# Choosing a core's program: the role read once and first, the two long programs swapped in place

## The reference

```python
def hybrid_layer(x, mem, g_in, w_in, g_q, g_kv, w_uq, w_ukv, sinks, rel_table,
                 g_mem, w_mem_kv, w_out, cos, sin):
    h = rms_norm(x, g_in)
    (c_q, c_kv, k_pe, z_mla, q_swa, k_swa, v_swa, z_swa, q_mem, z_mem) = split_cols(h @ w_in, IN_SIZES)
    y_mla = mla_attention(c_q, c_kv, k_pe, g_q, g_kv, w_uq, w_ukv, cos, sin) * jax.nn.silu(z_mla)
    y_swa = swa_attention(q_swa, k_swa, v_swa, sinks, rel_table) * jax.nn.silu(z_swa)
    y_mem = memory_attention(q_mem, rms_norm(mem, g_mem), w_mem_kv) * jax.nn.silu(z_mem)
    y = jnp.concatenate([y_mla, y_swa, y_mem], axis=-1) @ w_out  # (B, S, D_MODEL)
    return x + y
```

## Time and profile before

| | us |
|---|---|
| median of 3 runs | 723.43 (722.95 to 726.67) |
| the profiled execution, its own time | 723.23 |
| its span on the slowest core (core 2) | 721.7 |
| span of core 6, which has the same role | 720.5 |
| spans of the other six cores | 696.6 to 706.0 |
| PE busy on core 2 | 663.2 (92% of the span) |
| DVE, ACT, POOL busy on core 2 | 401.4, 404.0, 67.8 |

### The profile page before, as it was taken

The page is one execution under the profiler, slowest core; times in us unless marked ns, Lnnn a source line. Parts: engine busy times, 40 slices in busy tenths (PEclk is TensorE's granted clock), DMA queues, the critical chain, the costliest instruction groups (busy, mean ns, idle before and its releaser), DMA issues.

```text
span 721.7 us, 12773 instructions; the slowest of 8 cores (696.6 to 721.7 us)
## 1 busy us (share of the span) xinstructions
PE 663.2 (92%) x4313; PEld 371.2 (51%) x4313; DVE 401.4 (56%) x695; ACT 404.0 (56%) x640; POOL 67.8 (9%) x93
## 2 busy tenths in 40 slices
PE   0799868999999999999999899999999999999993
PEld 0345536766666644465564465464464464444441
DVE  0546343533553678657556664866766774334352
ACT  2236331240685888786578887787898862222221
POOL 2504020560010100100020000000000000000000
PEclk9999999999999999999999999999999999999997
DMA  8999999492059001828020001057039652512221
GB/s 182 217 250 221 196 208 176 104 168 45 0 96 183 9 5 30 157 50 207 0 64 23 1 2 33 1 100 151 16 49 191 229 188 77 175 59 95 81 89 63
DMA packets 19554, 75.61 MB, mean 105 GB/s; under 512 B 3208, under 2 KB 5320, under 8 KB 16784
## 3 DMA queue, kind: packets, MB, share of 16 engines
q0 software_dynamic: 9728, 44.86, 33.7%
q1 hardware_dynamic: 9744, 29.75, 12.1%
HBM read 100.05 MB, written 8.91 MB: 151 GB/s over the span
## 4 chain that ended last, share of the span: by engine, by line
PE 75%; DMA 10%; ACT 4%; issue 4%; DVE 3%; POOL 1%; POOLq 1%; SPq 0%; DVEq 0%; ACTq 0%
PE psd L705 75%; DMA w_r<-wmk 7%; DMA xs_r<-xu 3%; ACT pmb_r L670 2%; ACT rim_r L670 1%; POOLq L1925 1%; DVE acc_r L673 1%; POOL xs_r L211 1%; POOL w_r L211 0%; ACT V_r L687 0%; DVE accb_r L673 0%; POOLq L1924 0%; DVE p_r L673 0%; SPq L211 0%; DVE xo_r L673 0%
## 5 line engine op out<-in xcount | busy, mean ns | idle before, releaser
L705 PE MATMUL psd<-x_r,w_r 128*128 128x448 bf16 (+2 forms) x1344 | 215.3, 318 | 5.6 <-DVE kmT_r L673 3.1
L705 PEld LDWEIGHTS psd<-x_r,w_r 128*128 128x128 bf16 x1344 | 130.6, 98 | 84.2 <-issue 12.3
L670 ACT ACTIVATE pmb_r<-psd 128x768 bf16<-128x768 f32 (+3 forms) x156 | 129.0, 880 | 19.5 <-PE psd L705 17.5
L705 PE MATMUL psd<-Qn_r,K_r 128*128 128x256 bf16 (+3 forms) x400 | 81.6, 306 | 1.9 <-ACT pmb_r L670 1.0
L705 PE MATMUL psd<-pmb_r,V_r 128*128 128x256 bf16 (+3 forms) x400 | 70.8, 304 | 3.1 <-ACT pmb_r L670 2.4
L670 ACT ACTIVATE junk_r<-xo_r 128x512 f32<-128x512 f32 x34 | 21.4, 629 | 85.9 <-DVE xo_r L673 83.2
L705 PE MATMUL psd<-wo_r,gA_r 128*128 128x512 bf16 (+1 forms) x288 | 64.3, 379 | 1.2 <-ACT pmb_r L670 1.2
L705 PE MATMUL psd<-x_r,wkv_r 128*128 128x512 bf16 (+2 forms) x192 | 35.6, 346 | 24.2 <-DVE x_r L694 19.9
L673 DVE TENSOR_TENSOR p_r<-pmb_r,pmb_r 128x896 bf16<-128x896 bf16 (+2 forms) x64 | 38.7, 608 | 23.6 <-ACT pmb_r L670 19.6
L673 DVE TENSOR_TENSOR xo_r<-psd,xo_r 128x512 f32<-128x512 f32 x34 | 23.4, 689 | 49.5 <-PE psd L705 49.5
L705 PEld LDWEIGHTS psd<-pmb_r,V_r 128*128 128x128 bf16 x400 | 37.2, 98 | 25.3 <-issue 9.6
(11 more groups left out here) (147 smaller groups left out, 901.0 us busy)
## 6 DMA issues: line engine op xcount, KB each, us to landing
w_r<-wti POOLq DMA_DIRECT2D x28, 512.0 KB, 15.2
wo_r<-wo POOLq DMA_DIRECT2D x4, 2048.0 KB, 17.9
xo_r<-xo SPq DMA_DIRECT2D x8, 1024.0 KB, 12.3
out<-xo_r SPq DMA_DIRECT2D x14, 512.0 KB, 2.7
xs_r<-xu POOLq DMA_DIRECT2D x4, 1024.0 KB, 10.5
w_r<-wmk POOLq DMA_DIRECT2D x8, 512.0 KB, 33.9
x_r<-xu POOLq DMA_DIRECT2D x4, 1024.0 KB, 10.5
xs_r<-xu POOLq DMA_DIRECT2D x4, 768.0 KB, 28.5
```

Source lines behind the costliest of these rows:

```text
L670: self.P.op("act", lambda e: e.activation(out=out, in_=in_, func=func, **kw), reads, writes, 0.19 + n / 1200.0)
L705: ins = e.matmul(out, lhsT=l, rhs=r, start=s0, stop=s1, skip_group_check=True)
```

## The change

The role input now holds one number, the place of the core's role in the order of the programs, and `ROLE_AT` says which role's program stands at which place: role 1, role 0, role 2, role 3. Every engine reads one register, as the first thing it does, and only then come the ten common entries on POOL and the one on SP. Two branches still choose: `If_lt(at, 2)`, and in each half `If_eq`.

```diff
 ROLES = ((0, 1344), (1344, 1088), (2432, 896), (3328, 768))
 ROLE_OF = (0, 3, 1, 2)
+
+ROLE_AT = (1, 0, 2, 3)
 NMAX = 11
...
     def body(e, eng):
         n = FIRST.get(eng, 0)
-        hi, lo = e.alloc_register("hi_" + eng), e.alloc_register("lo_" + eng)
-        progs[0].replay(eng, e, 0, min(n, 4))
-        e.reg_load(hi, role_d[0:1, 0:1])
-        e.reg_load(lo, role_d[0:1, 1:2])
-        progs[0].replay(eng, e, min(n, 4), n)
-        with e.If_eq(hi, 0):
-            with e.If_eq(lo, 0):
-                progs[0].replay(eng, e, n, None)
+        at = e.alloc_register("at_" + eng)
+        e.reg_load(at, role_d[0:1, 0:1])
+        progs[0].replay(eng, e, 0, n)
+        with e.If_lt(at, 2):
+            with e.If_eq(at, 0):
+                progs[ROLE_AT[0]].replay(eng, e, n, None)
             with e.Else():
-                progs[1].replay(eng, e, n, None)
+                progs[ROLE_AT[1]].replay(eng, e, n, None)
         with e.Else():
-            with e.If_eq(lo, 0):
-                progs[2].replay(eng, e, n, None)
+            with e.If_eq(at, 2):
+                progs[ROLE_AT[2]].replay(eng, e, n, None)
             with e.Else():
-                progs[3].replay(eng, e, n, None)
+                progs[ROLE_AT[3]].replay(eng, e, n, None)
...
-            "swab": swab, "sinkr": sinkr, "hm": hm, "sel": sel, "role": np.array([[role // 2, role % 2]], np.int32),
+            "swab": swab, "sinkr": sinkr, "hm": hm, "sel": sel, "role": np.array([[ROLE_AT.index(role), 0]], np.int32),
```

## The result

The changed kernel takes 729.38 us (median of 6 runs, 728.21 to 730.31) against 723.8 us for the kernel before (6 runs). The ratio is 1.0068, 95% interval 1.0053 to 1.0082, so +4.9 us (3.8 to 5.9) of 723.8: slower, by more than the 0.5% that the prediction tells from no change. (The quotient of the two medians is 1.0077, +5.6 us; all ratios here are those on record, with their intervals, and not quotients of medians.) The forecast was +4.0 us, 727.2 us, with a range of 724.0 to 730.0. Measured a second time beside other kernels it was 1.0050 (1.0033 to 1.0067), +3.6 us. Now and then an execution of any of these kernels shows a lower granted clock on the cores of one die and takes some per cent longer; medians and ratios here leave such executions out.

The account below looks back on a forecast made before the run. Transfers bound cores 2 and 6 to about 110 us, then PE, then SP's tail. From 723.23 us, +1.4 (later first transfer) - 0.6 (hole closed) + 3.2 (exit jump) = +4.0, so 727.2 us; range 724.0 to 730.0.

Parts of the forecast that it names:

- What bounds the kernel: Cores 2 and 6: DMA transfers to about 110 us, then PE in fixed order keeping any loss, then SP's tail.
- The head start at the entry: PE on role 1's cores could begin some 6 us earlier, but waits for the same bytes: 0 us.
- The first rival: Transfers do not set the pace, PE keeps 4.9 us from the entry: 721.5 us, not slower; chance 5%.
- The first transfer is later: POOL reads the role ahead of its first transfer, so the DMA queue starts later: +1.4 us, far bound 6.4.
- The hole goes: POOL's eight transfers in one row remove the DMA dip at 17 to 19 us: -0.6 us on core 2.
- The entry as a whole: On core 2, +1.4 us for the later queue start and -0.6 us for the closed DMA dip.
- One more jump at the exit: SP on role 1's cores leaves by two branches, not one, with nothing hiding it: +3.2 us, bounds 2.6 to 3.8.
- The second rival: SP's extra exit branch costs only its own 0.04 us: sum +0.8, 724.1 us, no change; chance 10%.
- The others jump twice at their ends too, but were done several us ahead: At the exit, engines other than SP also jump twice, but finish several us earlier; no time was added for them.
- The sum: On core 2, +1.4 - 0.6 + 3.2 = +4.0 us, so 727.2 us; core 6 stays below core 2.
- a sign of being wrong: The PE stretch at 110.88 us moving by several us either way, or SP's last branch and drain staying 2.6 us apart.
- Rival 3: POOL's read at the entry takes 6.39 us, not 1.4, so the start is 5.0 us later: 732.2 us; chance 4%.

Follow-up runs that it names:

- the two runs with SP apart: Changed kernel, POOL's read behind its fourth entry; role 1's list last for SP, first for other engines: 719.87 us; the mirror: 723.89 us.

## Why the prediction was right

The time came out slower as forecast and inside the range; +4.0 us stood against +4.9 (3.8 to 5.9) and, measured again, +3.6. By its steps:

- *What bounds the kernel.* Right. Starting the queue 5.6 us later costs 4.0 to 5.3 us. From the start of the PE stretch near 110 us to the last four matmuls it is 595.9 to 598.8 us on cores 2 and 6 of every kept trace, so what a core lacks by then it still lacks at the end.
- *The head start at the entry is worth nothing.* Right. PE began at 13.44 us instead of 18.87 on core 2 and reached the stretch at 110 us at nearly the same time. With role 1 last it began at 20.31 us, and the time was the second best of all; the two runs with SP apart, 9 us apart at the start, end their matmuls together. The first rival falls.
- *The first transfer is later, +1.4 us.* Right in the read itself (1.42 us, the issue 1.47 us later). The move of the read alone costs 0.5 to 2.0 us, 1.4 in the mean of three pairs.
- *The hole goes, -0.6 us.* The hole went. Its size is less sure than the prediction has it: over 15 to 19 us the DMA share of core 2 before is 0.93, which makes 0.3 us and not 0.6. Taking away only the second read closes it too (1.02 at 17 to 19 us) and gave -0.9 us (-1.7 to 0), but that run took the second read from all engines, so the 0.9 is not the hole's alone. It needs no read ahead of the transfers.
- *The entry as a whole, +0.8 us.* Too high. The read first, alone, is this sum without the exit, and it gave -0.4 us (-1.2 to +0.5).
- *One more jump at the exit, +3.2 us.* Right in SP's own part: 5.6 and 5.7 us against 2.6 and 2.5 are 3.0 to 3.2. The second rival, an exit jump at the 0.04 us of its branch, falls: SP stands still for 2.5 to 3.1 us after each. The Trainium skill, "Advanced Engine Details and Errata", Control Flow Timing, gives about 51 ns for a branch that is always taken: that is near the 38 to 43 ns of SP's branch rows here, and not the price of such a jump. The term was too small as a whole, though: the tail grew by 3.7 us on core 2 and 4.0 on core 6. The step that fell short is "The others jump twice at their ends too, but were done several us ahead". They were, but their code came over the same DMA engines as the last outputs (the queue q14 has 7 packets behind 709 us on core 2 where only the others jump twice, 5 where only SP does, 12 in the changed kernel and 6 before), the outputs landed later, and SP's first exit branch came 0.7 us later behind the last matmul on both cores. That the fetches delay the outputs is shown by who jumps; in what way they do is not.
- *The sum.* An entry put too high and an exit put too low (by the tail) offset each other, so that +4.0 stands so near to +3.6 and +4.9 is in part luck. Core 2 lost 3.7 us, but all of it in the tail: its PE stretch came at 110.70 us and not at 111.7. Core 6, forecast to stay below core 2, lost 7.3 and set the time; 3.3 of it were there at 112.72 us, a shift of the kind that the prediction names as a sign of being wrong. The second profiled execution of the changed kernel does not repeat it: its PE stretches come at 108.50 and 109.34 us, its tails are 15.7 and 16.3 us. In the six runs of the changed kernel core 2's span went from 725.4 to 728.7 us and core 6's from 725.3 to 728.3. One execution of a core thus differs by some 3 us from another, and an entry term of 0.8 us cannot be read off one pair of traces. Why a single execution of a core is fast or slow in the transfers was not tried.
- *Rival 3, POOL reading slowly on an empty queue.* Falls: 1.42 us, and 1.36 us four times over.

What was to be had here lies the other way round: the slowest core's program last, so that it jumps at the entry, where transfers cover it, and not at the exit, where nothing does; and the read behind the transfers. That is 0.9939 of the kernel before, 719.28 us.

## What to carry to other kernels

Where one program holds several cores' programs, a jump is cheap at the entry if transfers are waited for there anyway, and dear at the exit, where every engine waits for the last one: put the slowest core's program last, so that it runs out into the end. An engine that issues the first transfers should issue some of those that need no decision before it reads anything, as most of each microsecond that the queue starts later comes back at the end when the queue is full for the first part of the run; whether four or all ten stand ahead made no difference that could be told here. And what other engines fetch beside the last outputs belongs to the tail, even if their own work is done.

## What the runs showed that I had not expected

A jump at the entry takes longer the more transfers it meets. In the run with one read in the old order PE's branch over role 0's program took this long (ns min/median/max, start us):

```profile
L1929 PEldq COMPARE_BRANCH  x1: 8247/8247/8247, 3.1 to 3.1; - x1
```

8.2 us on core 2 beside full transfers (a DMA share of 0.95 from 3.0 to 11.4 us), where SP's exit jumps take 2.5 to 3.2 us in all runs. That is another engine, but PE's jump over the programs of roles 0 and 1 can be seen on core 1 in two runs, with one read in the old order (DMA share 0.94 from 3 to 11 us) and with four more reads, where POOL's transfers start only behind 8 us (share 0.08 from 2.0 to 6.4 us):

```profile
L1928 PEldq COMPARE_BRANCH  x1: 7957/7957/7957, 3.0 to 3.0; - x1
L1930 PEldq COMPARE_BRANCH  x1: 3600/3600/3600, 2.8 to 2.8; - x1
```

So it is 8.0 us beside full transfers and 3.6 us with hardly any. The Trainium skill, "Runtime: NRT & Kernel Launch", Instruction fetch mechanics, has a taken branch to a place that is not held wait for a DMA fetch of its target. The rows agree, and show that the wait grows with the load. Why 3.6 us are still more than SP's at the exit is open: PE is another engine, and at the entry several engines jump at once. In the run with one read in the old order PE still began at 13.03 us on core 2 in place of 18.87, because with one read less it came to its jump at 3.1 us and not at 10.8. So most of the earlier start that the change gave to PE needed no swap, and it was worth at most the 0.9 us of that run.
